# Expert output biases summed once per token, and gathers that pass over padding slots, in a mixture-of-experts kernel

## The chip, the cores and the metric

The kernel runs on one core of a Trainium2 chip. The metric is the device time of one execution in microseconds (us); the lower the better. Three executions of the kernel before gave a median of 3492.59 us.

## The reference, cut to what matters

A 512-token sequence of width 1024 passes through two layers of one network and then one layer of another. The last stage of the second is a mixture of 32 experts, of which each token uses four:

```python
def moe_ffn(h, router_w, router_b, w1, b1, w2, b2):
    ...
    top_val, top_idx = lax.top_k(logits, TOP_K)
    gates = jax.nn.softmax(top_val, axis=-1)
    ...
    def run_block(args):
        toks, e = args
        hb = x_pad[toks] @ w1[e] + b1[e]
        g_part = jnp.minimum(hb[..., ::2], SWIGLU_LIMIT)
        u_part = jnp.clip(hb[..., 1::2], -SWIGLU_LIMIT, SWIGLU_LIMIT)
        act = g_part * jax.nn.sigmoid(SWIGLU_ALPHA * g_part) * (u_part + 1)
        return act @ w2[e] + b2[e]

    y_slots = lax.map(run_block, (slot_tok.reshape(n_blocks, MOE_BLOCK), block_exp))
    y_slots = y_slots.reshape(n_slots, shp[-1]) * slot_gate[:, None].astype(xt.dtype)
    out = jnp.zeros((t + 1, shp[-1]), xt.dtype).at[slot_tok].add(y_slots)[:t]
```

A block is 128 slots of one expert. 512 tokens times 4 experts fill 2048 slots. A block that isn't full has padding slots, whose gate is 0. The sum over a token's four experts of gate times `b2[e]` is a product of the token's row of 32 gates with `b2`.

## The kernel before, in words

Everything up to the experts is one long static program: two layers of mixers and feed-forward (PE reads weight tiles that SP streams into a ring of 8 slots, `ring`), then the second network's mixer, its output projection (`out2`), the router and the tables of the experts. The experts are a loop with one turn for each block of 128 slots, and a last block written out without the work for a next one (`expert_block(i, more)` on PE, ACT and DVE, `route` on POOL, `loads` on SP). All engines run their own instruction streams in order and meet at semaphores.

One turn handles 24 weight tiles of 128x1024 (512 KB each): 0 to 7 and 8 to 15 are the two halves of `w1`, 16 to 23 are `w2`. Each tile passes through four hands:

- SP loads it into its ring slot (L427) as soon as DVE has finished with the tile that was there 8 tiles earlier (`s_lo`).
- ACT rounds it into a high part (`round_tile`, L1673), once the tile has landed and once PE has used the tile 6 earlier (`s_freed`; there are `SPLITS` = 6 pairs of parts).
- DVE subtracts to get the low part (`rest_of_tile`, L2514).
- PE multiplies: high by high, high by low, low by high, each in two halves of 512 columns, six matmuls a tile (`product`, L1150).

ACT and DVE run ahead of PE by up to six tiles. Between the tiles, in an order that is written out by hand in each engine's `expert_block`, lies the rest of a turn:

- PE adds a bias to each of its three products by a matmul of `sel` (the one-hot of the expert) with `biases` (`bias`, L1140): `b1` in two halves at L1164 and L1170, and `b2` at L1177.
- DVE makes the activation for each half (`swiglu`, L2542 to L2551), ACT its sigmoid (L1696), PE transposes it (`act_turned`, L1158), ACT rounds the transposed half (`act_hi`, L1702), and DVE subtracts (`act_lo`, L2557). PE waits for the first half of `act_lo` before tile 16 (L1178) and for the second before tile 20 (L1190).
- POOL works out which rows of `x_rows` the next block needs, gathers them with an indirect DMA (`gather`, L495), makes the one-hot matrices `pick` (L558) and `sel` (L561, after PE's `y_bias`), and adds the finished block to `y_rows` with an indirect DMA (L565).
- PE transposes the gathered rows (`x_turned`, L1101, first half after a wait for the gather at L1185), ACT and DVE round and subtract them (L1724, L2577).
- At the end of its turn ACT copies the block's output out of the banks, times the gates (`y_kept`, L1732), once PE has done the last tile (L1728). ACT's first tile of the next turn follows after that.

Padding slots: `row_next` gives them a row number of 512 or more. `x_rows` has 1024 rows, of which the upper 512 are zeros, written once by SP (L416, behind a wait for DVE at L414); the gather fetches them. The scatter adds the padding slots' zeros to the upper half of `y_rows`.

The prologue of the experts loads the biases into rows 0 to 63 of `biases` (POOL L479), clears, rounds and subtracts them (DVE L2388, ACT L1648, DVE L2394). The epilogue adds, for each of eight 128-wide slices of the output (`sums`, L1203 to L1214), the last block (`y_slot` times `last_rows`) and the four token blocks of `y_rows`, transposed.

## Time and profile before

| what | us |
|---|---|
| median of three runs | 3492.59 |
| the three runs | 3491.3 to 3494.47 |
| the profiled execution, its own time | 3500.01 |
| its span in the trace | 3498.2 |
| experts' loop, first block's first matmul to the last `y_kept` | 2257.3 to 3460.9 |

The page of the profile gives for the whole span:

```profile
DVE  4774655554854646555548970499999999999996
PEclk9989999999989999999999999899999999999999
DMA  5111344321101343321120013399999999999995
GB/s 201 49 31 34 102 136 137 116 90 60 42 25 55 119 133 122 115 91 54 49 74 17 25 52 111 125 355 357 356 374 362 354 365 368 357 367 367 357 366 203
```

A digit is the busy share of one fortieth of the span (87 us) in tenths. The last third is the loop of the experts. The profiled execution's own time is 1.8 us above its span, and 7.4 us above the median of the three runs.

### The profile page before, as it was taken

To read this page: it belongs to the slowest core of one execution; us is meant where nothing else is said; L and a number is where in the kernel's file an instruction comes from. 1 tells how busy PE (TensorE), PEld (TensorE's weight loads), DVE (VectorE), ACT (ScalarE), POOL (GpSimd) and SP (SyncE) were. 2 spreads that over 40 slices of the span, in tenths; PEclk is the share of its full clock that TensorE was granted. 3 is DMA by queue.
4 is the path that set the end of the run, shared out by engine and by line. 5 is a ranking of instruction groups with operands and counts; after the bars stand their busy time and mean duration, and the time that the engine had idled before them with its cause. 6 is when DMAs were issued, how large, how long until landed. Compare 5 with 4: busy or idle time off the path is not lost.

```text
span 3498.2 us, 42721 instructions
## 1 busy us (share of the span) xinstructions
PE 3311.9 (95%) x13182; PEld 2291.0 (65%) x13182; DVE 2430.2 (69%) x2947; ACT 1686.2 (48%) x2237; POOL 490.5 (14%) x625
## 2 busy tenths in 40 slices
PE   8979999999889999989999989799999999999997
PEld 3454587774353777755645654587888778878875
DVE  4774655554854646555548970499999999999996
ACT  3432433232441423232221140388888888888884
POOL 0000000000000000000000000143343443343341
PEclk9989999999989999999999999899999999999999
DMA  5111344321101343321120013399999999999995
GB/s 201 49 31 34 102 136 137 116 90 60 42 25 55 119 133 122 115 91 54 49 74 17 25 52 111 125 355 357 356 374 362 354 365 368 357 367 367 357 366 203
DMA packets 168012, 618.33 MB, mean 177 GB/s; under 512 B 18528, under 2 KB 18656, under 8 KB 167328
## 3 DMA queue, kind: packets, MB, share of 16 engines
q1 hardware_dynamic: 157232, 573.90, 45.5%
q0 software_dynamic: 10672, 43.00, 4.3%
q8 instruction: 66, 1.08, 0.1%
q14 instruction: 42, 0.34, 0.0%
HBM read 587.99 MB, written 28.84 MB: 176 GB/s over the span
## 4 chain that ended last, share of the span: by engine, by line
PE 72%; DVE 15%; issue 5%; ACT 3%; DMA 3%; DVEq 0%; POOL 0%; ACTq 0%; SPq 0%; POOLq 0%
PE bank L592 53%; PE bank L1150 16%; DVE w_part L2514 5%; DMA sb_ring<-in_w 3%; DVE sb_rstd L1770 1%; DVE sb_work L1808 1%; DVE sb_work L2547 1%; PE bank L1140 1%; DVE sb_work L2542 1%; ACT w_part L1673 1%; DVE sb_work L2544 1%; PE bank L1101 1%; PE bank L1158 1%; DVE sb_work L1956 0%; DVE sb_work L2270 0%
## 5 line engine op out<-in xcount | busy, mean ns | idle before, releaser
L2514 DVE TENSOR_TENSOR w_part<-sb_ring,w_part 128x1024 fp32r<-128x1024 f32 x762 | 890.4, 1225 | 66.1 <-ACT w_part L1673 65.4
L1673 ACT ACTIVATE w_part<-sb_ring 128x1024 fp32r<-128x1024 f32 x762 | 771.1, 1053 | 84.6 <-PE bank L1150 44.4
L1150 PE MATMUL bank<-w_part,xg_hi 128*128 128x512 f32 x2048 | 564.3, 397 | 0.0
L592 PE MATMUL bank<-h_hi,split_part 128*128 128x512 f32 x1408 | 445.0, 401 | 7.9 <-ACT h_hi L1431 7.9
L1150 PEld LDWEIGHTS bank<-w_part,xg_hi 128*128 128x128 f32 x2048 | 383.2, 188 | 88.8
L592 PE MATMUL bank<-sb_work,sb_ring 128*128 128x512 f32 (+2 forms) x840 | 315.4, 532 | 10.6 <-DVE sb_work L1786 10.6
L1150 PE MATMUL bank<-w_part,xg_lo 128*128 128x512 f32 x1024 | 321.3, 395 | 0.0
L592 PEld LDWEIGHTS bank<-h_hi,split_part 128*128 128x128 f32 x1408 | 266.4, 190 | 80.0 <-issue 15.6
L1150 PE MATMUL bank<-w_part,act_hi 128*128 128x512 f32 x1024 | 285.0, 400 | 1.7 <-DVE act_lo L2557 0.6
L592 PE MATMUL bank<-sb_hT,sb_ring 128*128 128x512 f32 x576 | 265.4, 619 | 11.7 <-ACT sb_hT L1251 11.7
L592 PE MATMUL bank<-h_lo,split_part 128*128 128x512 f32 x704 | 272.7, 394 | 0.0
L592 PEld LDWEIGHTS bank<-sb_work,sb_ring 128*128 128x128 f32 (+1 forms) x840 | 159.2, 192 | 156.7 <-issue 137.3
L592 PE MATMUL bank<-act_hi_ff,split_part 128*128 128x512 f32 x704 | 229.3, 407 | 5.7 <-DVE act_lo_ff L2129 5.7
L1424 ACT ACTIVATE split_part<-sb_ring 128x1024 fp32r<-128x1024 f32 x136 | 142.7, 1052 | 178.0 <-PE bank L592 178.0
L592 PE MATMUL bank<-sb_work 128*128 128x64 f32 (+7 forms) x1000 | 195.4, 400 | 31.2 <-DVE sb_work L2005 16.6
L1150 PEld LDWEIGHTS bank<-w_part,xg_lo 128*128 128x128 f32 x1024 | 192.8, 188 | 46.3
L592 PEld LDWEIGHTS bank<-sb_hT,sb_ring 128*128 128x128 f32 x576 | 114.4, 200 | 159.7 <-issue 157.6
L1150 PEld LDWEIGHTS bank<-w_part,act_hi 128*128 128x128 f32 x1024 | 187.6, 188 | 45.1 <-issue 4.1
L1481 ACT ACTIVATE sb_work<-bank 128x512 f32<-128x512 f32 x88 | 52.7, 599 | 310.5 <-PE bank L592 296.9
L592 PE MATMUL bank<-sb_xT,sb_ring 128*128 128x512 f32 (+2 forms) x416 | 181.5, 619 | 11.7 <-ACT sb_xT L1251 11.7
L592 PEld LDWEIGHTS bank<-sb_work 128*128 128x128 f32 (+3 forms) x1000 | 127.8, 207 | 82.6 <-issue 21.9
L2087 DVE TENSOR_TENSOR split_part<-sb_ring,split_part 128x1024 fp32r<-128x1024 f32 x136 | 165.9, 1221 | 19.5 <-ACT split_part L1424 19.1
(357 smaller groups left out, 4477.3 us busy)
## 6 DMA issues: line engine op xcount, KB each, us to landing
sb_ring<-in_w SPq DMA_DIRECT2D x768, 512.0 KB, 7.9
sb_ring<-in_wstream SPq DMA_DIRECT2D x304, 512.0 KB, 3.5
y_rows<-sb_padc POOLq DMA_DIRECT2D x1, 4096.0 KB, 17.5
sb_xT<-in_x SPq DMA_DIRECT2D x4, 512.0 KB, 6.8
x_rows<-sb_padc SPq DMA_DIRECT2D x1, 2048.0 KB, 10.2
residual<-sb_hT POOLq DMA_DIRECT2D x1, 2048.0 KB, 6.5
sb_hT<-residual POOLq DMA_DIRECT2D x1, 2048.0 KB, 8.1
x_rows<-sb_work SPq DMA_DIRECT2D x1, 2048.0 KB, 7.0
```

The costliest lines, as they stand in the source:

```text
L592: ins = nc.tensor.matmul(out, l, r, start=start, stop=stop)
L1101: ins = nc.tensor.transpose(out[:, k * P:(k + 1) * P], block_rows[:, (half * 4 + k) * P:(half * 4 + k + 1) * P], ident)
L1140: ins = nc.tensor.matmul(out[n][:], sel, biases[:, at + n * 512:at + (n + 1) * 512], start=True, stop=False)
L1150: ins = nc.tensor.matmul(out[n][:], l[:, k, :], r[:, n * 512:(n + 1) * 512], start=False, stop=(k, p) == (KD - 1, 2))
L1158: ins = nc.tensor.transpose(banks[6 + half][:, k * P:(k + 1) * P], u_part[:, half, k * P:(k + 1) * P], ident)
L1424: nc.scalar.activation(split_hi[t % NSPLIT], ring[:, n % RING, :], ACT.Copy).then_inc(act_done, did.up(("w_hi", l, t)))
L1481: nc.scalar.activation(ubuf[:, i % 4, 1:T + 1], bank_of("up", l, c, v)[:], ACT.Copy).then_inc(act_done, did.up(("free", "up", l, c, v), (" ...
L1673: nc.scalar.activation(w_hi[t % SPLITS], ring[:, t % RING, :], ACT.Copy).then_inc(s_hi, 1)
L1770: nc.vector.reciprocal(out, out).then_inc(dve_done, did.up())
L1808: nc.vector.scalar_tensor_tensor(out=dst[c], in0=a, scalar=b, in1=dst[c], op0=ALU.mult, op1=ALU.add).then_inc(dve_done, did.up())
L2087: nc.vector.tensor_tensor(split_lo[t % NSPLIT], ring[:, n % RING, :], split_hi[t % NSPLIT].bitcast(F32), ALU.subtract).then_inc(dve_done, ...
L2514: nc.vector.tensor_tensor(w_lo[t % SPLITS], ring[:, t % RING, :], w_hi[t % SPLITS].bitcast(F32), ALU.subtract).then_inc(s_lo, 1)
```

## The change

`b2` leaves the blocks. PE's bias matmuls of the third product go, and its first matmul starts the banks instead; POOL's `sel` waits for the second half of `b1` (`up_bias`) where it waited for `y_bias`. `b2` is loaded four times, into the four groups of 32 partitions of `b2_rows`. In the prologue PE transposes the gates (16 matmuls of 32 columns by 128, `gates_turned`), ACT copies them to `gate_t`. In the epilogue eight matmuls of 32 rows (`output_bias`) put gates times `b2` into the eight sums, six of them ahead of the wait for the last block, two at `m == 4`. Each uses one of the four groups of 32 rows.

The gather gets a bounds check at row 511, with rows beyond it left out and no error. So the zero rows of `x_rows`, their DMA, and the two waits for it go; POOL clears `block_rows` once before the loop. The last block, the scatter and `y_rows` stay as they are.

```diff
-ROWS_X = 2 * T
+ROWS_Y = 2 * T
...
-        biases = parts("biases", 1, 3 * D)[:, 0, :]
+        biases = parts("biases", 1, 2 * D)[:, 0, :]
+        b2_rows = region(D)
...
-        last_rows = turn_tables[:, 0, :]
+        last_rows, gate_t = turn_tables[:, 0, :], turn_tables[:, 1, :]
...
-                if n == RING + 1:
-                    sp.wait_ge(dve_done, when("zeros"))
-                    zeros = padc[:].rearrange("p a t -> p (a t)")[:, 0:D]
-                    sp.dma_start(x_rows[T:, :].rearrange("(g p) d -> p g d", p=P),
-                                 zeros.unsqueeze(1).to_broadcast([P, ROWS_X // P - TB, D])).then_inc(s_zero, 16)
...
             for half in range(2):
-                for at, name, n in ((0, "b1", 2 * D), (2 * D, "b2", D)):
-                    pool.dma_start(biases_raw[half * 32:half * 32 + 32, at:at + n], io[name]).then_inc(s_bias, 16)
+                pool.dma_start(biases_raw[half * 32:half * 32 + 32, :], io["b1"]).then_inc(s_bias, 16)
+            for i in range(P // EXPERTS):
+                pool.dma_start(b2_rows[i * EXPERTS:(i + 1) * EXPERTS, :], io["b2"]).then_inc(s_b2, 16)
...
                 nc.gpsimd.indirect_dma_start(out=block_rows, out_offset=None, in_=x_rows[:, :],
-                    in_offset=bass.IndirectOffsetOnAxis(ap=idx_next, axis=0)).then_inc(s_got, 16)
+                    in_offset=bass.IndirectOffsetOnAxis(ap=idx_next, axis=0), bounds_check=T - 1,
+                    oob_is_err=False).then_inc(s_got, 16)
...
-            pool.wait_ge(s_zero, 16)
             pool.wait_ge(s_rows, 16)
             pool.wait_ge(dve_done, when("biases"))
+            nc.gpsimd.memset(block_rows, 0.0).then_inc(pool_done, did.up(("block_rows_cleared",)))
+            pool.wait_ge(pool_done, did.n)
...
-                    pool.wait_ge(moe_pe_done, in_turn(i, "y_bias", more=more))
+                    pool.wait_ge(moe_pe_done, in_turn(i, "up_bias", more=more))
...
+            pe.wait_ge(dve_done, when("gates"))
+            for b in range(TB):
+                for i in range(P // EXPERTS):
+                    ins = nc.tensor.matmul(banks[3][i * EXPERTS:(i + 1) * EXPERTS, b * P:(b + 1) * P], gate[:, b, :],
+                                           ident, start=True, stop=True)
+            ins.then_inc(pe_done, did.up(("gates_turned",)))
...
+            pe.wait_ge(act_done, when("gates_kept"))
...
-                            ins = nc.tensor.matmul(out[n][:], l[:, k, :], r[:, n * 512:(n + 1) * 512], start=False,
-                                                   stop=(k, p) == (KD - 1, 2))
+                            ins = nc.tensor.matmul(out[n][:], l[:, k, :], r[:, n * 512:(n + 1) * 512],
+                                                   start=start and p == 0, stop=(k, p) == (KD - 1, 2))
...
-                bias(banks[2:4], D)
+                bias(banks[2:4], D).then_inc(moe_pe_done, turn_did.up(("up_bias",)))
...
                 pe.wait_ge(moe_act_done, in_turn(i, "y_kept", 1, back=1))
-                bias(banks[4:6], 2 * D).then_inc(moe_pe_done, turn_did.up(("y_bias",)))
                 pe.wait_ge(moe_dve_done, in_turn(i, "act_lo", 0, more=more))
                 for k in range(3):
-                    product(2 * KD + k, act_hi, act_lo, banks[4:6], k)
+                    product(2 * KD + k, act_hi, act_lo, banks[4:6], k, start=k == 0)
...
+            def output_bias(m):
+
+                r = slice(m % 4 * EXPERTS, (m % 4 + 1) * EXPERTS)
+                mm(outs[m][:], b2_rows[r, m * P:(m + 1) * P], gate_t[r, :], True, False)
+
+            pe.wait_ge(s_b2, 16 * (P // EXPERTS))
+            state["job"] = 0
+            outs = [bank("sums", m) for m in range(KD)]
+            for m in (0, 1, 2, 3, 6, 7):
+                output_bias(m)
             pe.wait_ge(dve_done, when("last_rows"))
-            state["job"] = 0
             for m in range(KD):
-                out = bank("sums", m)
+                out = outs[m]
                 if m % 4 == 0:
                     pe.wait_ge(moe_act_done, in_turn(last, "y_kept", m // 4, more=False))
-                mm(out[:], y_slot[:, m * P:(m + 1) * P], last_rows, True, False)
+                if m == 4:
+                    output_bias(4)
+                    output_bias(5)
+                mm(out[:], y_slot[:, m * P:(m + 1) * P], last_rows, False, False)
...
+            act.wait_ge(pe_done, when("gates_turned"))
+            nc.scalar.activation(gate_t, banks[3], ACT.Copy).then_inc(act_done, did.up(("gates_kept",)))
...
-                dve.wait_ge(s_zero, 16)
                 dve.wait_ge(s_put, 16)
```

The clearing, rounding and subtracting of `biases` (DVE L2388, ACT L1648, DVE L2394) shrink from 3072 to 2048 columns.

## Rows read from the trace of the kernel before

**Rows 1.** The page, part 1: busy time of each engine over the span.

```profile
PE 3311.9 (95%) x13182; PEld 2291.0 (65%) x13182; DVE 2430.2 (69%) x2947; ACT 1686.2 (48%) x2237; POOL 490.5 (14%) x625
```

**Rows 2.** Two turns as windows: length, busy PE, PEld, DVE, ACT, POOL, PEclk, DMA, GB/s.

```profile
2484.96:2523.42 38.46, 37.78 (x172) 30.14 (x171) 35.23 (x37) 30.76 (x37) 16.43 (x19) 1.00 0.97 353
2523.42:2560.49 37.07, 37.07 (x172) 30.25 (x171) 35.27 (x37) 30.92 (x37) 14.53 (x19) 1.00 1.00 372
```

**Rows 3.** Timeline of ACT (start, length, idle before), L1732, first and last of 32 pairs.

```profile
2297.03 1.25 ACT L1732 ACTIVATE sb_work<-bank,sb_work 128x512 f32<-128x512 f32 x2
...
3459.65 1.26 ACT L1732 ACTIVATE sb_work<-bank,sb_work 128x512 f32<-128x512 f32 x2 [7.18 <-PE bank L1150]
```

**Rows 4.** Timeline of PE in the shorter turn, around tile 20 and the turn's end.

```profile
2551.48 0.60 PE L1101 MATMUL bank<-sb_consts,sb_work 128*128 128x128 f32 x4
2551.84 1.18 PE L1150 MATMUL bank<-w_part,act_hi 128*128 128x512 f32 x4
...
2553.32 0.60 PE L1101 MATMUL bank<-sb_consts,sb_work 128*128 128x128 f32 x4
2553.67 1.19 PE L1150 MATMUL bank<-w_part,act_hi 128*128 128x512 f32 x4
...
2559.32 0.62 PE L1140 MATMUL bank<-biases,sel 128*128 128x512 f32 x2
2559.78 1.10 PE L1150 MATMUL bank<-w_part,xg_hi 128*128 128x512 f32 x4
```

**Rows 5.** Timeline of DVE in the shorter turn: first tile, second `act_lo`, last six tiles.

```profile
2527.07 8.04 DVE L2514 TENSOR_TENSOR w_part<-sb_ring,w_part 128x1024 fp32r<-128x1024 f32 x7 [1.47 <-ACT w_part L1673]
...
2552.86 0.68 DVE L2557 TENSOR_TENSOR act_lo<-bank,act_hi 128x512 fp32r<-128x512 f32 x1
...
2555.78 6.89 DVE L2514 TENSOR_TENSOR w_part<-sb_ring,w_part 128x1024 fp32r<-128x1024 f32 x6
```

**Rows 6.** Timeline of ACT in the shorter turn: `y_kept`, tile 12, the next `y_kept`.

```profile
2523.42 1.25 ACT L1732 ACTIVATE sb_work<-bank,sb_work 128x512 f32<-128x512 f32 x2
...
2532.67 1.06 ACT L1673 ACTIVATE w_part<-sb_ring 128x1024 fp32r<-128x1024 f32 x1 [0.33 <-PE bank L1150]
...
2560.49 1.25 ACT L1732 ACTIVATE sb_work<-bank,sb_work 128x512 f32<-128x512 f32 x2
```

**Rows 7.** Timeline of the longer turn: ACT's `y_kept`, tile 12, then DVE, PE at tile 20.

```profile
2484.96 1.25 ACT L1732 ACTIVATE sb_work<-bank,sb_work 128x512 f32<-128x512 f32 x2
...
2495.87 1.06 ACT L1673 ACTIVATE w_part<-sb_ring 128x1024 fp32r<-128x1024 f32 x1 [1.99 <-DMA sb_ring<-in_w]
...
2515.78 0.68 DVE L2557 TENSOR_TENSOR act_lo<-bank,act_hi 128x512 fp32r<-128x512 f32 x1
...
2516.59 1.19 PE L1150 MATMUL bank<-w_part,act_hi 128*128 128x512 f32 x4
```

**Rows 8.** POOL's gather in the shorter turn, and issue to landing of all 31.

```profile
2542.16 1.76 POOL L495 DMA_INDIRECT sb_work<-x_rows,sb_work  x1 [0.48 <-issue]
...
DMA to landing us min/median/max: 7.4/8.3/9.0
```

**Rows 9.** DMA: the gather's queue in 2504:2514, then all queues' slices in 2512:2522.

```profile
q0 software_dynamic: 144, 0.52, 13.1%
...
DMA  9999998989999998979999666698788446788998
```

**Rows 10.** PE's matmuls of 32 rows in 0:400, by shape: busy us, mean ns.

```profile
L592 PE MATMUL bank<-sb_work,sb_ring 32*128 32x512 f32 x4 | 2.0, 614 | 0.0
...
L592 PE MATMUL bank<-sb_work 32*128 32x384 f32 x16 | 1.9, 533 | 0.0
```

**Rows 11.** Timeline of PE at the end of the last block and the first sum.

```profile
3458.83 0.63 PE L1150 MATMUL bank<-w_part,act_lo 128*128 128x512 f32 x2
3460.39 1.13 PE L592 MATMUL bank<-sb_turn_tables,sb_work 128*128 128x512 f32 x2 [0.94 <-ACT sb_work L1732]
```

**Rows 12.** Timeline of PE: its first matmul of the experts' loop.

```profile
2257.34 1.22 PE L1140 MATMUL bank<-biases,sel 128*128 128x512 f32 x2 [7.39 <-POOL sb_work L530]
```

More of the change, by code:

```diff
@@ L149, in build @@
         s_bias = sem("expert_biases_loaded")
-        s_zero = sem("token_rows_cleared")
+        s_b2 = sem("output_biases_loaded")
         s_rows = sem("token_rows_stored")
@@ L169, in build @@
         banks = [bank_pairs[i // 2][:, i % 2 * 512:(i % 2 + 1) * 512] for i in range(8)]
-        x_rows = nc.dram_tensor("x_rows", (ROWS_X, D), F32, kind="Internal").ap()
-        y_rows = nc.dram_tensor("y_rows", (ROWS_X, D), F32, kind="Internal").ap()
+        x_rows = nc.dram_tensor("x_rows", (T, D), F32, kind="Internal").ap()
+        y_rows = nc.dram_tensor("y_rows", (ROWS_Y, D), F32, kind="Internal").ap()
         residual = nc.dram_tensor("residual", (P, KD * T), F32, kind="Internal").ap()
@@ L338, in build @@
         u_part = rows(2, D // 2)
-        biases_raw = work[:, raw_at:raw_at + 3 * D]
+        biases_raw = work[:, raw_at:raw_at + 2 * D]
         idents = region(EXPERTS)
@@ L432, in _ @@
                 sp.wait_ge(act_done, when("h2_row", b, 1))
-            sp.dma_start(x_rows[0:T, :].rearrange("(b p) d -> p b d", p=P), h2[:]).then_inc(s_rows, 16)
+            sp.dma_start(x_rows.rearrange("(b p) d -> p b d", p=P), h2[:]).then_inc(s_rows, 16)
             sp.wait_ge(dve_done, when("table"))
@@ L461, in _ @@
                            padc[:].rearrange("p a t -> p (a t)")[:, 0:D].unsqueeze(1).to_broadcast(
-                               [P, ROWS_X // P, D])).then_inc(s_put, 16)
+                               [P, ROWS_Y // P, D])).then_inc(s_put, 16)
             did = Count("pool", found)
@@ L1142, in bias, with product @@
                     return ins
-                def product(t, left_hi, left_lo, out, k):
+                def product(t, left_hi, left_lo, out, k, start=False):
                     pe.wait_ge(s_lo, i * MOE_TILES + (t + 1))
@@ L1643, in _ @@
                     c)).then_inc(act_done, did.up(("free", "yt", c), ("mixed", c)))
-            act.wait_ge(s_bias, 64)
+            act.wait_ge(s_bias, 32)
             act.wait_ge(dve_done, when("biases_cleared"))
-            nc.scalar.activation(biases[0:64, :], biases_raw[0:64, :], ACT.Copy).then_inc(act_done, did.up(("biases_hi",)))
+            nc.scalar.activation(biases[0:64, 0:2 * D], biases_raw[0:64, :], ACT.Copy).then_inc(act_done, did.up(("biases_hi",)))
             for k in range(KD):
@@ L2387, in _ @@
             dve.wait_ge(pe_done, when("full", "yt", XC - 1))
-            nc.vector.memset(biases.bitcast(F32), 0.0).then_inc(dve_done, did.up(("biases_cleared",)))
+            nc.vector.memset(biases[:, 0:2 * D].bitcast(F32), 0.0).then_inc(dve_done, did.up(("biases_cleared",)))
             for m in range(KD):
@@ L2393, in _ @@
                     dve.wait_ge(act_done, when("biases_hi"))
-                    nc.vector.tensor_tensor(biases[32:64, :], biases_raw[32:64, :], biases[32:64, :].bitcast(F32),
+                    nc.vector.tensor_tensor(biases[32:64, 0:2 * D], biases_raw[32:64, :], biases[32:64, 0:2 * D].bitcast(F32),
                         ALU.subtract).then_inc(dve_done, did.up(("biases",)))
@@ L2440, in _ @@
             nc.vector.tensor_tensor(gate, gate, gate_sum.unsqueeze(2).to_broadcast([P, TB, EXPERTS]),
-                ALU.mult).then_inc(dve_done, did.up())
+                ALU.mult).then_inc(dve_done, did.up(("gates",)))
             dve.wait_ge(pe_done, when("full", "rank"))
```

## The prediction, made before the changed kernel was run

> **What bounds the kernel now.** The page's busy times come first. PE looks like the bound, 95% of the span, with DVE far behind [rows 1]. That is a mean over stages with other limits, so the next view is windows of exactly one turn of the experts' loop, from one `y_kept` to the next [rows 2]. The reader is to see that turns come in two kinds, 37.07 and 38.46 us long, with the same work in them. The loop's mean lies between: from the first pair of `y_kept` to the last are 31 turns in 3459.65 - 2297.03 = 1162.62 us, 37.50 each [rows 3]. In the shorter turn PE is busy for all of the 37.07 us, but DVE for 35.27, and DMA's share is 1.00: three resources are near their end at once, and busy shares can't tell which one sets the turn. The timelines can.
>
> PE, shorter turn [rows 4]: before tile 20 PE transposes the second half of the gathered rows at 2553.32 and starts tile 20 at 2553.67, 0.35 later. The transposes of the first half, which have no wait behind them, take 2551.84 - 2551.48 = 0.36. So PE reached tile 20 without waiting.
>
> DVE, shorter turn [rows 5]: it idles once, 1.47 us, before the turn's first tile at 2527.07 (3.65 after `y_kept`, since ACT has the copy and a tile to do first). From there to the end of the last group at 2562.67 the timeline shows no idle time. In this unbroken chain the second `act_lo`, for which tile 20 waits, ends at 2552.86 + 0.68 = 2553.54. PE's tile 20 starts 0.13 behind it.
>
> The same pair in the longer turn [rows 7]: `act_lo` ends at 2515.78 + 0.68 = 2516.46, tile 20 starts at 2516.59, again 0.13 behind. And from the end of `act_lo` to the next `y_kept` it is 2560.49 - 2553.54 = 6.95 us in the shorter turn [rows 5, 6] and 2523.42 - 2516.46 = 6.96 in the longer [rows 6, 7]. **So both turns are timed by DVE's chain**: `y_kept`, ACT's first tile, DVE's unbroken work up to the second `act_lo` (30.12 us), then 6.95 us of four tiles on PE, ACT's last tile and `y_kept`. In the shorter turn PE arrives at the same moment by its own road.
>
> What makes a turn longer: ACT's tile 12 starts 10.91 us after `y_kept`, behind a wait of 1.99 for DMA, where it stands at 9.25 in the shorter turn [rows 6, 7]. 1.66 late, less a little slack, comes out as 1.39 in the turn. Over the loop such lateness is 37.50 - 37.07 = 0.43 a turn, 13.3 us in 31 turns.
>
> **The change, part by part.**
>
> *The two bias matmuls of the third product.* A pair takes 2559.78 - 2559.32 = 0.46 us of PE [rows 4], 14.3 us over 31 turns, more than the whole of the 0.2% (7 us) that a measurement of this kernel can tell from no change. But they stand before tile 16, and PE's time before tile 20 is what the DVE chain covers. Without them PE arrives at tile 20 at 2553.21 instead of 2553.67 and waits for an `act_lo` that is ready at 2553.54 and lets it start at 2553.67 as before. For the gain to get through, DVE's chain would have to start or run earlier. Its start is anchored to `y_kept`, its tiles up to 21 need only parts that PE frees before the place of the removed pair, and it has no idle time to give back. I take 0.01 a turn, -0.3 us; the bounds are 0 and -14.3. The last block has a wait of its own at tile 20 and gives nothing.
>
> Matmul busy time, read alone, names PE as the bound [rows 2]. The Trainium skill (Perfetto Trace Analysis, Identifying the Most-Contended Engine) calls that a bad measure, since matmuls are pipelined, and goes by weight loads for PE and by occupancy for the others, of which the highest is to be worked on first. By the first reading the sum here would be -14; by the rule DVE, at 35.27 of 37.07 against 30.25 for weight loads [rows 2], is the engine to relieve, and the removal on PE gives 0.
>
> *The gather.* `sel` waits for `up_bias` instead of `y_bias`, eight tiles earlier on PE; POOL makes it behind the four `pick`s, so an earlier signal frees nothing: 0, and a `sel` made sooner would be used no sooner. The gather was issued at 2542.16 and used at 2551.48 [rows 4, 8], 9.32 later; it lands 8.3 after issue, 9.0 at most [rows 8]. PE now comes for it 0.46 sooner, but may be held until the old moment without cost, since it only waits at tile 20 anyway. 2048 of 4096 slots are filled, so half of the rows go. The queue's 0.52 MB took 13.1% of 16 engines for 10 us, 1.31 us [rows 9]; half is 0.65 us of DMA a turn. What could that buy? Only the 13.3 us of late tiles. The lateness sits at tile 12, 8 to 11 us into a turn, beside the scatter. The gather is issued 2542.16 - 2523.42 = 18.7 us into the turn and lands at 27, when little is left before the second `act_lo` at 30. Between that place and the next tile 12 the DMA engines have slack: from about 2517.5 on, 6 us before the `y_kept` at 2523.42, quarters of a microsecond fall to 4 to 7 tenths [rows 9]. Backlog is worked off there, and 0.65 us less of it mostly widens a gap. I take -1 us; bounds 0 and -13.3.
>
> *Prologue.* PE waits 7.39 us before the loop's first matmul [rows 12]. In it fit 16 short transposes; from the pace of 0.09 us of the 128-column transposes (0.36 for four, [rows 4]) that is 1.5 us, and ACT's copy of 512 columns under 0.7 us (a `y_kept` pair is 1.25, [rows 6]). Both end before POOL's one-hots. POOL's clear of `block_rows` stands after the work that PE waits for, and 15 us before its next wait on ACT ends. The two more loads, the smaller `biases` and the missing 2 MB of zeros lie beside PE work that runs on: 0, bounds -1 and +1.
>
> *Epilogue.* PE idles 0.94 us before the first sum [rows 11], and from there to the end PE's work is the path. The six `output_bias` ahead of it: where matmuls of 32 rows use one group of rows, four of 512 columns take 2.0 us, 0.5 each; where four groups follow each other, sixteen of 384 columns take 1.9, 0.12 each [rows 10]. The new ones cycle through the groups. Side by side: four of 512 columns in 4 x 0.12 x 512/384 = 0.64, two more in 0.5: 1.14, less 0.94: +0.2. Two at `m == 4`: +0.5. Sum **+0.7**. One after another: 6 x 0.5 - 0.94 + 2 x 0.5 = +3.1, the upper bound; the lower is +0.3, with the six hidden and the last two side by side. I take +0.7, since the rows with different groups are the same pattern.
>
> **Sum**: -0.3 - 1 + 0 + 0.7 = -0.6 us on the profiled execution's 3500.01, so 3499.4. That execution lies 7.4 above the median of the runs, 3492.59; on the median it is **3492.0 us**.
>
> **The rivals.**
>
> *A, PE bounds the turn.* For it: PE 37.07 busy of 37.07, and no wait at tile 20 in the short turns. Against it: the constant 6.95 behind `act_lo` in turns of both kinds. It would give 3492.6 - 14.3 + 0.7 = 3479.0.
>
> *B, the lighter gather takes away the late tiles.* For it: DMA's share is 1.00 in the short turn, and lateness is all that makes turns longer. Against it: the slack between gather and tile 12. If two thirds of the 13.3 go: 3492.6 - 9 + 0.7 = 3484.
>
> *C, slower: the checked gather lands too late.* POOL computes the addresses in software, and the check may lengthen that. The margin is 9.32 - 8.3 = 1.0 us from issue to use [rows 4, 8]; past it every microsecond delays tile 19, tile 20 and the turn, and 31 turns make 31 us. If it lands 2 us later than now less the 0.65 saved, the turn loses 0.35: 3492.6 + 11 + 0.7 = 3504. From 1.65 us of added address work on it decides. Against it: half of the rows are gone, and the whole gather instruction is only 1.76 us on POOL.
>
> *D, the change doesn't do what it says*: rows out of bounds still cost a packet each. Then the gather's part is 0 instead of -1, and the time is 3493.0, inside the forecast.
>
> **How the numbers follow.** Forecast with D: 0.63 for within 0.2% (3485.6 to 3499.6). A 0.08 and B 0.16, both on the faster side, of B some that falls short of 7 us but about as much luck from late tiles falling elsewhere: faster 0.24. C 0.08, and 0.05 for more late tiles, since tile 12 is decided by tenths of a microsecond: slower 0.13. The range reaches down to most of B and leaves out A, 3481; and up to the serial epilogue with a few more late turns, 3499. The forecast's own range is 3489 to 3496.
>
> **What would show it.** Short turns still 37.05 to 37.07 long; in them PE now waits some 0.4 us at tile 20 for DVE's `act_lo`, a wait that the page before doesn't show there; 6.95 us from `act_lo` to `y_kept`; no L1140 of the third product; half of the gather's packets; the same number of turns with tile 12 late; first sum 0.2 later. Wrong if short turns fall to 36.6 (A), if long turns vanish (B), or if PE waits at the gathered rows (C).

## The result, and the profile after

The changed kernel takes 3500.52 us (median of 8 runs, 3496.07 to 3510.85), the kernel before on the same chip 3492.86 (8 runs): ratio 1.0026, interval 1.0014 to 1.0038, 7.7 us slower. The prediction was 3492.0, in a range from 3481 to 3499: the kernel is slower than that, by 8.5 us against the forecast and 1.5 against the end of the range. The same kernel as a new program gave 1.0022 (1.0013 to 1.0031).

The changed kernel's page, engines' busy times (as [rows 1]), the software queue, the third product's group:

```profile
PE 3306.4 (95%) x13166; PEld 2275.4 (65%) x13166; DVE 2426.6 (69%) x2947; ACT 1685.9 (48%) x2238; POOL 502.0 (14%) x628
...
q0 software_dynamic: 10768, 35.04, 3.8%
...
L1156 PE MATMUL bank<-w_part,act_hi 128*128 128x512 f32 x1024 | 285.1, 400 | 3.7 <-DVE act_lo L2575 0.9
```

The reader is to see that the group of the expert products (L1156) now has a wait for DVE's `act_lo`, which is that of tile 20. For queue 0 the DMA view of the whole execution is of use, the kernel before first:

```profile
DMA packets 168012, 618.33 MB, mean 177 GB/s; under 512 B 18528, under 2 KB 18656, under 8 KB 167328
q0 software_dynamic: 10672, 43.00, 4.3%
```

```profile
DMA packets 167580, 608.27 MB, mean 174 GB/s; under 512 B 20552, under 2 KB 20680, under 8 KB 166896
```

Queue 0 moved 35.04 MB where it had moved 43.00, so the bytes of the padding rows are gone. Its packets are not: 10672 before, 10768 now, and 2024 more of all packets are under 512 bytes, about the 1984 rows that 31 gathers skip at 64 each. A skipped row is still a packet, of 4 bytes in the trace and 9 ns where a row of 4 KB takes 164. A gather takes 0.69 us of the 16 engines instead of 1.32.

Three turns of the changed kernel as windows, columns as [rows 2]:

```profile
2447.33:2485.65 38.32, 37.31 (x170) 29.74 (x169) 35.23 (x37) 30.87 (x37) 15.78 (x19) 1.00 0.98 354
2485.65:2522.73 37.08, 36.98 (x170) 29.79 (x169) 35.22 (x37) 31.15 (x37) 16.23 (x19) 1.00 1.00 356
2522.73:2559.81 37.08, 36.98 (x170) 29.80 (x169) 35.23 (x37) 31.12 (x37) 16.54 (x19) 1.00 1.01 366
```

The short turn is 37.08 as before, with two matmuls fewer. Its PE timeline, answering [rows 4], and behind it DVE's line for the second `act_lo` [rows 5]:

```profile
2550.44 0.60 PE L1100 MATMUL bank<-sb_consts,sb_work 128*128 128x128 f32 x4
2550.80 1.19 PE L1156 MATMUL bank<-w_part,act_hi 128*128 128x512 f32 x4
...
2552.29 0.60 PE L1100 MATMUL bank<-sb_consts,sb_work 128*128 128x128 f32 x4
2552.99 1.19 PE L1156 MATMUL bank<-w_part,act_hi 128*128 128x512 f32 x4
```

```profile
2552.18 0.68 DVE L2575 TENSOR_TENSOR act_lo<-bank,act_hi 128x512 fp32r<-128x512 f32 x1
```

From the second transposes to tile 20 it is 0.70 us now, 0.35 before, and 0.36 behind the first transposes: PE arrives earlier and waits 0.34, until 0.13 behind the end of `act_lo`, as predicted.

A longer turn is as before too: tile 12 waits for its DMA and starts 10.77 behind `y_kept`, as in [rows 7]. Timeline of ACT:

```profile
2447.33 1.25 ACT L1751 ACTIVATE sb_work<-bank,sb_work 128x512 f32<-128x512 f32 x2
...
2458.10 1.06 ACT L1690 ACTIVATE w_part<-sb_ring 128x1024 fp32r<-128x1024 f32 x1 [1.49 <-DMA sb_ring<-in_w]
```

First and last `y_kept`, as [rows 3]:

```profile
2295.88 1.25 ACT L1751 ACTIVATE sb_work<-bank,sb_work 128x512 f32<-128x512 f32 x2
...
3457.46 1.26 ACT L1751 ACTIVATE sb_work<-bank,sb_work 128x512 f32<-128x512 f32 x2 [7.17 <-PE bank L1156]
```

The loop is 1161.58 us here, 1162.62 in the profiled execution before. This says little: the number of long turns differs from execution to execution (below), and both spans happen to be 3498.2. The prologue ends 1.15 us sooner here and 0.92 later in the repetition (first `y_kept` at 2297.95); over all runs below that moment moves between 2295.1 and 2299.0, so no cost shows. The final sums tell more. PE's timeline there, against [rows 11]:

```profile
3457.19 3.05 PE L591 MATMUL bank<-sb_turn_tables,sb_work 32*128 32x512 f32 x14
3460.09 1.05 PE L591 MATMUL bank<-sb_consts,sb_work 128*128 128x128 f32 x8
...
3465.34 1.02 PE L591 MATMUL bank<-sb_turn_tables,sb_work 128*128 128x512 f32 x2
3466.20 1.05 PE L591 MATMUL bank<-sb_consts,sb_work 128*128 128x128 f32 x8
...
3468.04 2.18 PE L591 MATMUL bank<-sb_turn_tables,sb_work 32*128 32x512 f32 x6
3470.06 1.05 PE L591 MATMUL bank<-sb_consts,sb_work 128*128 128x128 f32 x8
```

A token-row matmul (two records) takes 3466.20 - 3465.34 = 0.86 to its follower. With six `output_bias` ahead of it the same step takes 2.90: 2.04 for six, 0.34 each. With two it takes 2.02: 1.16 for two, 0.58 each. The output's DMA, by SP's timeline, the kernel before first:

```profile
3491.55 0.34 SPq L453 DMA_DIRECT2D out_h<-sb_xT  x1
```

```profile
3491.53 0.34 SPq L449 DMA_DIRECT2D out_h<-sb_xT  x1
```

From the last `y_kept` to it: 3491.55 - 3459.65 = 31.90 before, 3491.53 - 3457.46 = 34.07 after. This stretch is called the tail below. **The final sums cost 2.17 us**, in every profiled execution alike (34.07 or 34.08 with all eight output biases there, 31.89 or 31.90 without). That leaves 5.5 of the 7.7 us.

### The profile page after: what moved, and what is told of

Its sections match the earlier page's. It is cut to its first block, busy times and chain, and to the rows that moved or that the text cites. A ratio compares the mean times of both kernels' runs of the same rounds, so it can differ in the third digit from the quotient of the medians.

```text
span 3498.2 us, 42721 instructions
## 1 busy us (share of the span) xinstructions
PE 3306.4 (95%) x13166; PEld 2275.4 (65%) x13166; DVE 2426.6 (69%) x2947; ACT 1685.9 (48%) x2238; POOL 502.0 (14%) x628
## 3 DMA queue, kind: packets, MB, share of 16 engines
q0 software_dynamic: 10768, 35.04, 3.8%
## 4 chain that ended last, share of the span: by engine, by line
PE 64%; DVE 19%; issue 8%; DMA 4%; ACT 4%; DVEq 0%; POOL 0%; ACTq 0%; SPq 0%; POOLq 0%
PE bank L591 52%; PE bank L1156 9%; DVE w_part L2532 7%; DMA sb_ring<-in_w 4%; DVE sb_rstd L1789 1%; DVE sb_work L1827 1%; DVE sb_work L2565 1%; ACT w_part L1690 1%; DVE sb_work L2560 1%; DVE sb_work L2562 1%; DVE act_lo L2575 0%; DVE sb_work L2288 0%; DVE sb_work L1974 0%; DVE sb_work L2332 0%; PE bank L1100 0%
## 5 line engine op out<-in xcount | busy, mean ns | idle before, releaser
L1156 PE MATMUL bank<-w_part,xg_hi 128*128 128x512 f32 x2048 | 564.1, 397 | 0.0
L1156 PEld LDWEIGHTS bank<-w_part,xg_hi 128*128 128x128 f32 x2048 | 383.2, 188 | 89.2
L591 PE MATMUL bank<-sb_work,sb_ring 128*128 128x512 f32 (+2 forms) x840 | 315.4, 531 | 10.6 <-DVE sb_work L1805 10.6
L1156 PE MATMUL bank<-w_part,xg_lo 128*128 128x512 f32 x1024 | 321.2, 395 | 0.0
L1156 PE MATMUL bank<-w_part,act_hi 128*128 128x512 f32 x1024 | 285.1, 400 | 3.7 <-DVE act_lo L2575 0.9
L1156 PEld LDWEIGHTS bank<-w_part,xg_lo 128*128 128x128 f32 x1024 | 192.6, 188 | 46.5
L1156 PEld LDWEIGHTS bank<-w_part,act_hi 128*128 128x128 f32 x1024 | 187.4, 188 | 50.8 <-issue 9.8
```

Of the source, the lines that this page charges most:

```text
L591: ins = nc.tensor.matmul(out, l, r, start=start, stop=stop)
L1156: ins = nc.tensor.matmul(out[n][:], l[:, k, :], r[:, n * 512:(n + 1) * 512], start=start and p == 0, stop=(k, p) == (KD - 1, 2))
```

## The experiments

Each ratio is against the kernel before on the same chip, beside the runs compared. "Loop" is first to last `y_kept` of the profiled execution, "long" its turns over 37.9 us of 31, "DMA" what ACT idled for a tile's DMA in the loop (in the line that rounds tiles).

| kernel | median us | ratio, interval | loop | long | DMA us |
|---|---|---|---|---|---|
| before (first profile) | 3492.86 | | 1162.6 | 9 | 36.4 |
| after (first profile) | 3500.52 | 1.0026 (1.0014-1.0038) | 1161.6 | 8 | 30.7 |
| again_before | 3496.34 | 0.9999 (0.9990-1.0008) | 1157.4 | 4 | 28.4 |
| again_after | 3502.41 | 1.0022 (1.0013-1.0031) | 1157.1 | 5 | 25.3 |
| check_only | 3496.98 | 1.0002 (0.9993-1.0011) | 1163.6 | 9 | 36.2 |
| check_only_again | 3500.50 | 1.0019 (1.0010-1.0028) | 1166.5 | 11 | 38.4 |
| bias_only | 3497.49 | 1.0009 (0.9998-1.0021) | 1164.2 | 11 | 32.2 |
| bias_only_again | 3497.49 | 1.0009 (1.0000-1.0019) | 1155.4 | 3 | 25.1 |
| after_pe_filled | 3502.43 | 1.0027 (1.0016-1.0038) | 1156.5 | 4 | 23.7 |
| after_no_sums_bias | 3499.58 | 1.0018 (1.0007-1.0028) | 1165.6 | 11 | 34.5 |
| before_no_scatter | 3485.22 | 0.9978 (0.9969-0.9987) | 1147.8 | 0 | none |
| after_no_scatter | 3482.45 | 0.9968 (0.9959-0.9978) | 1142.7 | 0 | none |
| before_scatter_checked | 3495.60 | 1.0005 (0.9996-1.0014) | 1159.1 | 7 | 17.0 |
| after_scatter_checked | 3496.44 | 1.0008 (0.9999-1.0018) | 1159.6 | 7 | 21.1 |
| before_scatter_late | 3488.33 | 0.9982 (0.9973-0.9991) | 1149.7 | 0 | 10.6 |
| after_scatter_late | 3490.79 | 0.9978 (0.9968-0.9988) | 1150.6 | 0 | 14.4 |
| before_lo_early | 3504.60 | 1.0027 (1.0015-1.0039) | 1161.7 | 4 | 55.9 |
| after_lo_early | 3508.70 | 1.0034 (1.0022-1.0047) | 1170.7 | 13 | 71.6 |
| after_lo_early_bias_moved | 3502.02 | 1.0026 (1.0015-1.0038) | 1166.9 | 8 | 70.2 |
| after_lo_early_scatter_late | 3542.96 | 1.0115 (1.0094-1.0136) | 1222.2 | 15 | 14.9 |

**Chance first.** again_before and again_after are the two kernels unchanged.

> The kernel before, once more, for a second profile of it. Its first profile was of an execution of 3500.0 us, above all eight timed ones (3486.7 to 3494.5). If that was chance, this profile shows a loop some 5 to 7 us shorter than 1162.6, with fewer turns over 37.9 us than the 9 of 31. If profiling itself costs the time, it shows about 3500 again. Ratio 1.000.

> The changed kernel, once more, for a second profile. Ratio to the kernel before 1.002 to 1.003 as measured (7 to 9 us). If the added time is the epilogue and more late turns: y_kept of the last block to the output's DMA 34.1 us again (31.9 before), and 8 or more turns over 37.9 us, shortest turns 36.9 to 37.1.

The first came as expected. Of the second the ratio and the tail did (34.08), but 5 turns are long where 8 or more were expected. Two executions of one and the same kernel have loops 3 to 9 us apart in the table. So one profiled execution can't show 5 us; medians of some ten runs can, and so can kernels without long turns.

**The two halves.** check_only is the kernel before with the bound on the gather:

```diff
-                    in_offset=bass.IndirectOffsetOnAxis(ap=idx_next, axis=0)).then_inc(s_got, 16)
+                    in_offset=bass.IndirectOffsetOnAxis(ap=idx_next, axis=0), bounds_check=T - 1,
+                    oob_is_err=False).then_inc(s_got, 16)
...
+            nc.gpsimd.memset(block_rows, 0.0).then_inc(pool_done, did.up(("block_rows_cleared",)))
```

> The kernel before with the bounds check of the gather and the clearing of block_rows alone; biases stay in the blocks. If the partial gather is what costs (its rows sit on fewer DMA engines, so that tiles finish less evenly): slower by 4 to 6 us, with more late turns. If the gather is harmless as I predicted: within 2 us of before, rather faster by 1.

> The kernel before with the bound on the gather alone, once more, because its first 12 runs (1.0002, 0.9993 to 1.0011) can't tell 1 us from 4. If the lighter gather carries the rest of the loss, 1.001 or more; if it costs nothing, 0.999 to 1.0005.

bias_only is the kernel after with the old gather:

```diff
-                    in_offset=bass.IndirectOffsetOnAxis(ap=idx_next, axis=0), bounds_check=T - 1,
-                    oob_is_err=False).then_inc(s_got, 16)
+                    in_offset=bass.IndirectOffsetOnAxis(ap=idx_next, axis=0)).then_inc(s_got, 16)
...
-            nc.gpsimd.memset(block_rows, 0.0).then_inc(pool_done, did.up(("block_rows_cleared",)))
```

> The changed kernel with the gather as it was (all rows, zero rows in x_rows). If the bias part is what costs: all of the 7 to 8 us, of which 2.2 is the epilogue and -1 the prologue, the rest in the loop, though its shortest turns are no longer than before. If it is the gather: +1 to +2 us, the epilogue alone.

> The kernel after with the gather unchecked over 1024 rows as before, once more (first 1.0009, 0.9998 to 1.0021). If the bias part carries the whole loss, 1.002 or more; if it is the final sums alone, 1.0006.

The bias half costs 0.0009 twice, 3.1 us, of which the final sums are 2.2. The gather half gave 0.0002 and 0.0019, on different chips: 0.7 and 6.6 us, and the two intervals barely meet, at 0.0010. With their mean, about 4, the halves add up to 7, what the change costs. But on the chip where both halves and the whole were run side by side they add up to 0.0011 against 0.0022 for the whole. How the loss divides between the halves isn't settled.

**Is it PE's earlier arrival?** after_pe_filled puts two matmuls of the removed form back (`sel` waits for `y_bias` again):

```diff
                 pe.wait_ge(moe_act_done, in_turn(i, "y_kept", 1, back=1))
+                for n in range(2):
+                    ins = nc.tensor.matmul(banks[4 + n][:], sel, biases[:, n * 512:(n + 1) * 512], start=True, stop=True)
+                ins.then_inc(moe_pe_done, turn_did.up(("y_bias",)))
```

> The kernel after with two matmuls of the removed form (sel against 512 columns of biases) put back at the old place of the third product; their result is thrown away by the start of tile 16, so that only their 0.46 us on PE and the old signal for sel are restored. Theory 1 (PE's earlier arrival changes the order of work around it and with that the number of turns with a late tile 12): the 4 to 5 us that the final sums don't explain go, ratio 1.0006 to 1.0012. Theory 2 (they come from the lighter gather or the prologue, or were chance): ratio stays at 1.0018 to 1.0026.

1.0027, where theory 1 had 1.0006 to 1.0012: it falls. With PE's time and the old signal restored the loss is still there, so PE's earlier arrival isn't what costs. after_no_sums_bias leaves the eight `output_bias` out:

```diff
-            for m in (0, 1, 2, 3, 6, 7):
-                output_bias(m)
...
-                if m == 4:
-                    output_bias(4)
-                    output_bias(5)
-                mm(out[:], y_slot[:, m * P:(m + 1) * P], last_rows, False, False)
+                mm(out[:], y_slot[:, m * P:(m + 1) * P], last_rows, True, False)
```

> This kernel leaves out the eight output_bias matmuls of the final sums, so the output biases are in no output; all else is the kernel after. Theory (the final sums carry a third of the loss): from the last y_kept to the output's DMA issue 31.9 us as before instead of 34.1, and the ratio 1.0022 falls by 2.2 / 3493 = 0.0006 to about 1.0016. Rival (the final sums carry it all, since each ran alone in the earlier runs by chance): the ratio falls to 1.000. If it stays at 1.0022 or more, the tail is not what a slower run shows.

The tail is 31.90 again. The ratio, 1.0018 (1.0007 to 1.0028), is clear of the rival's 1.000; 0.0006 less than before is inside its interval and can't be told from no gain.

**Taking the scatter away.** Both kernels, the scatter-add replaced by a DMA of 64 bytes:

```diff
-                    nc.gpsimd.indirect_dma_start(out=y_rows[:, :], out_offset=bass.IndirectOffsetOnAxis(ap=idx_cur,
-                        axis=0), in_=y_slot, in_offset=None, compute_op=ALU.add).then_inc(s_put, 16)
+                    pool.dma_start(y_rows[0:1, 0:16], y_slot[0:1, 0:16]).then_inc(s_put, 16)
```

> This kernel leaves out the scatter-add of each block's output to the token rows (a DMA of 64 bytes takes its place, so that the waits stay), so only the last block's outputs reach the sums; all else is the kernel before. Theory (turns are longer than 37.07 us only where the scatter gets ahead of tile 12): every turn 37.07 to 37.1, the loop 31 x 37.08 = 1149.5 us against 1157 to 1164, the time 8 to 13 us less, ratio 0.9965 to 0.998, and the spread between executions shrinks to a few us. Rival (late tiles come from DMA's load as such): long turns stay.

> The same leaving out of the scatter-add on the kernel after. Theory 1 (of the 7 us that the change costs, 2.2 are the final sums and the rest are more or longer late turns): 2.2 us over before_no_scatter, and no more. Theory 2 (something in the prologue or the short turns that the profiles don't show costs the rest): 7 us over before_no_scatter, as with the scatter.

The first expectation held. Of the second neither theory did: both have the changed kernel slower. Of all runs these tell the most. No turn is long, and the spread is 3 us instead of 12 to 15. Without the scatter the changed kernel is the **faster** one, by 3485.22 - 3482.45 = 2.8 us. The loops differ by 1147.8 - 1142.7 = 5.1 in its favour, the final sums by 2.2 against it. Timelines show why, first before_no_scatter: DVE's second `act_lo`, PE's second transposes, tile 20.

```profile
2512.36 0.68 DVE L2556 TENSOR_TENSOR act_lo<-bank,act_hi 128x512 fp32r<-128x512 f32 x1
...
2512.99 0.60 PE L1100 MATMUL bank<-sb_consts,sb_work 128*128 128x128 f32 x4
...
2513.35 1.18 PE L1149 MATMUL bank<-w_part,act_hi 128*128 128x512 f32 x4
```

`act_lo` has ended at 2513.04; tile 20 starts 0.31 later, 0.36 behind the transposes: PE doesn't wait, it sets this turn of 37.07. The same in after_no_scatter:

```profile
2511.56 0.68 DVE L2574 TENSOR_TENSOR act_lo<-bank,act_hi 128x512 fp32r<-128x512 f32 x1
2511.73 0.60 PE L1099 MATMUL bank<-sb_consts,sb_work 128*128 128x128 f32 x4
...
2512.37 1.19 PE L1155 MATMUL bank<-w_part,act_hi 128*128 128x512 f32 x4
```

Tile 20 stands 0.13 behind `act_lo`, so DVE sets a turn of 36.90. Its `act_lo` ends 2512.24 - 2482.29 = 29.95 behind `y_kept`; with the scatter it is 2552.86 - 2522.73 = 30.13. So with the scatter DVE's chain is 0.18 longer (in before_no_scatter it is 2513.04 - 2483.09 = 29.95 too), and that is just what hid PE's gain: the kernel before sat on a tie of two engines at 37.07.

The scatter therefore costs the kernel before about 8 us (3493.21 - 3485.22), all of it in turns over 37.07. For the kernel after the runs with it were on other chips, so the ratios are used: 1.0026 or 1.0022 less 0.9968, 19 to 20 us, of which 31 x 0.18 = 5.6 are in the short turns and 13 to 15 in longer ones. **By this account the change pays 5 to 7 us more in turns that are longer than the short ones.** It is an account by elimination, from medians: the single profiled executions don't show it, with 8 and 5 long turns in the kernel after and 9 and 4 in the kernel before.

**A lighter scatter.** Both kernels with `bounds_check=T - 1, oob_is_err=False` on the scatter-add too.

> The kernel after with the bound T - 1 on the scatter-add too, so that padding slots are passed over in both. Theory (scatter beside tile 12): the scatter's 2.64 us of 16 DMA engines fall to 1.3, fewer turns are late, the time falls by 3 to 10 us against the kernel after: ratio 0.9995 to 1.0015 against before. Rival (the address work on POOL or the number of rows doesn't matter): 1.0024 as the kernel after.

> The kernel before with the bound T - 1 on the scatter-add alone (the gather stays whole). Theory: 3 to 10 us less than the kernel before, ratio 0.997 to 0.999, faster than both kernels, since it has the lighter scatter and not the 2.2 us in the final sums. Rival: no difference.

Half of the scatter's rows gone: the kernel after gains 5 to 6 us by the ratios, as expected, the kernel before nothing, where 3 to 10 us were expected. 7 turns of 31 are still long in both, inside the 4 to 9 of the kernels with the whole scatter. ACT's waits for DMA do fall, from 28.4 and 36.4 us to 17.0 in the kernel before. So half the bytes take away waits, but not the long turns.

**A later scatter.** Three one-column additions on POOL ahead of it, in either kernel:

```diff
+                    for _ in range(3):
+                        after(turn_did, 3, (moe_pool_done, own_turn(i, turn_did)))
                     nc.gpsimd.indirect_dma_start(out=y_rows[:, :], out_offset=bass.IndirectOffsetOnAxis(ap=idx_cur,
```

> The kernel before with three more one-column additions on POOL ahead of the scatter-add, which is then issued 1 us later (3.4 us into the turn instead of 2.4), DVE and PE unchanged. Theory (the slower lo_early kernels are slower because their scatter is issued at 3.0 to 3.5 and meets tile 12 more often): ratio 1.001 to 1.003, more turns over 37.5. Rival (the moment of issue doesn't matter): 1.000.

> The kernel after with the same three additions on POOL ahead of the scatter-add. Theory (what the change costs beyond the final sums comes only through turns whose tile 12 falls behind the scatter): issued 0.9 us later, the scatter lets tile 12 pass in nearly every turn, and what remains between this kernel and before_scatter_late is the final sums: 3488.3 + 2.2 = 3490.5, ratio 0.9988 to 0.999, spread of a few us. Rival (the lighter gather costs 4 us by another way): 3494 or more, ratio 1.000.

The first expectation has the wrong sign: issued later, the scatter does *less* harm. POOL's timeline in the kernel before, `y_kept` at 2523.42:

```profile
2524.75 0.90 POOL L504 TENSOR_TENSOR sb_work<-sb_work 128x1 f32<-128x1 f32 x1 [11.11 <-ACT sb_work L1732]
2525.81 1.65 POOL L565 DMA_INDIRECT y_rows<-sb_work  x1 [0.16 <-POOL sb_work L504]
```

And in before_scatter_late, `y_kept` at 2518.69:

```profile
2520.02 1.71 POOL L504 TENSOR_TENSOR sb_work<-sb_work 128x1 f32<-128x1 f32 x4 [11.12 <-ACT sb_work L1734]
2522.02 1.65 POOL L567 DMA_INDIRECT y_rows<-sb_work  x1 [0.29 <-issue]
```

Issue moves from 2.39 to 3.33 behind `y_kept`. The load that tile 12 waits for is issued by SP at the same place in both, 1.22 behind `y_kept`; before, then before_scatter_late:

```profile
2524.64 0.33 SPq L427 DMA_DIRECT2D sb_ring<-in_w  x1
```

```profile
2519.91 0.33 SPq L427 DMA_DIRECT2D sb_ring<-in_w  x1
```

So its head start on the scatter is 1.17 us before and 2.11 here. ACT's group for the tiles in 2300:3435 (busy, mean, idle before and its releasers), of before, before_no_scatter, before_scatter_late:

```profile
L1673 ACT ACTIVATE w_part<-sb_ring 128x1024 fp32r<-128x1024 f32 x727 | 735.4, 1053 | 78.5 <-PE bank L1150 39.4 <-DMA sb_ring<-in_w 36.4
```

```profile
L1672 ACT ACTIVATE w_part<-sb_ring 128x1024 fp32r<-128x1024 f32 x736 | 738.8, 1052 | 59.1 <-PE bank L1149 58.0
```

```profile
L1675 ACT ACTIVATE w_part<-sb_ring 128x1024 fp32r<-128x1024 f32 x734 | 741.8, 1053 | 64.1 <-PE bank L1152 51.4 <-DMA sb_ring<-in_w 10.6
```

The DMA entry is the lateness: 36.4 with the scatter at 2.4, none without it, 10.6 with it at 3.3, and no long turn is left. So it is a race of the scatter with tile 12: from issue to landing the load of tile 12 takes 6.5 to 9.8 us in the kernel before, over 8 in 11 turns of 31; 6.5 to 7.7 without the scatter; 6.0 to 7.8 with the later one. ACT can take the tile 9.26 behind `y_kept`, 8.03 behind the load's issue. In that setting the changed kernel takes 3490.79 (3490.5 was expected) and the unchanged one 3488.33. Their difference, 2.5, fits the final sums, but they ran on different chips; by the ratios the changed kernel is 1.4 us the faster, give or take some 5. What the pair shows is that the loss beyond the sums is gone or small. Both are faster than the kernel before, by 0.9978 (0.9968 to 0.9988) and 0.9982 (0.9973 to 0.9991), and compute all of it.

**An earlier `act_lo`.** DVE makes the second `act_lo` one tile sooner:

```diff
-                for t in range(2 * KD + SPLITS - 1, 2 * KD + SPLITS + 1):
-                    rest_of_tile(i, t)
-                rest_of_act(1)
-                rest_of_tile(i, 2 * KD + SPLITS + 1)
+                rest_of_tile(i, 2 * KD + SPLITS - 1)
+                rest_of_act(1)
+                for t in range(2 * KD + SPLITS, 2 * KD + SPLITS + 2):
+                    rest_of_tile(i, t)
```

> Theory (DVE's chain to the second act_lo times the short turns, and the removal of the third product's bias on PE is real but covered by it): with the second act_lo one tile earlier on DVE it no longer waits behind 1.2 us of tile 21 and 22, only for ACT's act_hi, some 0.6 us earlier. PE's wait of 0.4 at tile 20 goes, short turns fall from 37.06 to 36.6 to 36.7, and 31 turns give 10 to 14 us: ratio 0.997 to 0.999 against the kernel before, where the kernel after has 1.0022. Rival (DMA times the turn): short turns stay at 37.0, ratio 1.002.

> The same reordering on the kernel before. Theory: there PE arrives at tile 20 as late as DVE, with 37.06 us of work of its own in the turn, so act_lo earlier gives at most 0.1 a turn: short turns 36.9 to 37.06, ratio 0.999 to 1.000. Rival (DVE alone sets it, PE has slack): as much as in the kernel after, ratio 0.996.

after_lo_early_bias_moved also has, in the last block:

```diff
                 product(2 * KD + 3, act_hi, act_lo, banks[4:6], 3)
+                if not more:
+                    for m in range(4):
+                        output_bias(m)
```

> after_lo_early with the output biases of the first four row groups issued in the last block, ahead of PE's wait at tile 20. Theory: at 0.41 us each they cost PE 1.6 us there less what is left of that wait (0.3 to 0.9), and the first sum starts behind two of them instead of six, inside its wait for y_kept: 1 us or less under after_lo_early, tail from y_kept 32.9 instead of 34.1. Rival: they shift the last block by as much as they save, no difference.

Windows of a longer and a short turn of after_lo_early:

```profile
2485.15:2523.48 38.33, 37.03 (x170) 29.70 (x169) 35.32 (x37) 30.98 (x37) 15.30 (x19) 1.00 0.96 340
2523.48:2560.21 36.73, 36.73 (x170) 29.77 (x168) 35.56 (x37) 30.87 (x36) 15.03 (x19) 1.00 1.01 376
```

The shortest turns are near what the theory said: 36.73 with the change, 37.06 without it. This settles the tie. Removing PE's pair alone leaves the short turns at 37.08, an earlier `act_lo` alone at 37.07, and both together give 36.73. The times are not what it said, for ACT's waits for a tile's DMA double (71.6 and 55.9 us). DVE ends its turn later and frees the slot for tile 12 later; POOL's small addition is held as well, 1.83 us where it had taken 0.90. After_lo_early, `y_kept` at 2485.15, first SP's load of tile 12, then POOL:

```profile
2487.30 0.33 SPq L423 DMA_DIRECT2D sb_ring<-in_w  x1
```

```profile
2486.48 1.83 POOL L502 TENSOR_TENSOR sb_work<-sb_work 128x1 f32<-128x1 f32 x1 [10.73 <-ACT sb_work L1751]
2488.47 1.64 POOL L564 DMA_INDIRECT y_rows<-sb_work  x1 [0.16 <-POOL sb_work L502]
```

The scatter goes out at 3.32, as late as in before_scatter_late, but the load goes out at 2.15, and its head start is 1.17 again. With it the load takes 6.1 to 9.8 us, over 8 in 11 turns, as in the kernel before (before_lo_early: up to 10.3, over 8 in 4 turns). So, as far as these profiles show, what the load suffers goes by the distance of the two issues, and not by the scatter's own moment. And since ACT still wants the tile at 9.26, a load that leaves 0.92 later is late more often: in 25 turns of 31, against 11.

Moving four biases saved 0.9 us of the tail (33.2; 32.9 was expected). The medians fell by 6.7 us and the ratio by 0.0008, 2.8 us, which is within its interval: the tail alone shows what the move gives.

after_lo_early_scatter_late adds the three additions to that.

> after_lo_early_bias_moved with the three additions ahead of the scatter-add. Theory (there the short turns are 36.75 to 36.85, and only the late tiles hid that; with the scatter out of tile 12's way they show): loop 31 x 36.9 = 1144 us, tail 33, time 3482 to 3486, ratio 0.997, faster than every other version that computes all. Rival (with turns of 36.8 the scatter, now issued 4.3 us in, meets the next tiles or the DMA engines are full): ratio 1.000 or more.

1.0115, the worst of all. POOL's timeline in a turn whose `y_kept` is at 2533.40, then PE's:

```profile
2534.74 3.60 POOL L502 TENSOR_TENSOR sb_work<-sb_work 128x1 f32<-128x1 f32 x4 [10.72 <-ACT sb_work L1757]
2538.49 2.45 POOL L566 DMA_INDIRECT y_rows<-sb_work  x1 [0.16 <-POOL sb_work L502]
...
2556.59 1.91 POOL L492 DMA_INDIRECT sb_work<-x_rows,sb_work  x1
```

```profile
2564.92 0.93 PE L1102 MATMUL bank<-sb_consts,sb_work 128*128 128x128 f32 x4 [3.77 <-DMA sb_work<-x_rows,sb_work]
```

Four additions take 3.60 us instead of 1.71: DVE idles only 0.54 there, and 1.48 in before_scatter_late. The scatter leaves at 5.09, the next gather at 23.2 instead of 18.9, and PE waits 3.77 for its rows: a turn of 42.15. This is rival C's mechanism, a gather that lands too late. In the loop PE waits 51.2 us in all for gathered rows here, and 0.3 or less in every other run.

## Why the prediction was wrong, point by point

- *The third product's bias, 0 to -0.3 us in the loop*: right for this kernel, short turns 37.08 and a wait of 0.34 at tile 20. "Both turns are timed by DVE's chain" was true by hundredths only, so the right number owes something to luck. Without the scatter the old turn is PE's, 37.07, and the removal gives 0.17 a turn. Rival A was half there. The Trainium skill's advice to work on the engine with the highest occupancy (Perfetto Trace Analysis, Identifying the Most-Contended Engine) picks DVE, and the removal on PE gave nothing, as it has it; but relieving DVE alone gave nothing either (before_lo_early), and in before_no_scatter, where DVE is still the busier by that measure, the engine to relieve is PE.
- *What starts DVE's chain*: "3.65 after `y_kept`, since ACT has the copy and a tile to do first" leaves out a term. Between the two stands a load of ACT's function tables, in the shorter turn of the kernel before:

```profile
2524.68 1.28 ACT L1673 ACT_TABLE_LOAD   x1
```

  It doesn't change the forecast, since it is there in both kernels, but these 1.28 us are part of DVE's chain in 30 of 31 turns. No run takes them away.
- *The lighter gather, -1 us, bounds 0 and -13.3*: **this step failed.** It is the only term that priced the late tiles, and its bounds allowed no loss. Measured, the change loses some 5.5 us beyond the final sums. With the scatter gone it gains 5.1 in the loop instead, and with a later scatter the loss is gone or small. The gather alone gave +0.7 and +6.6. The reasoning "0.65 us less of it mostly widens a gap" concerned the mean load, but lateness is the outcome of a race decided by tenths of a microsecond, and a change of DMA timing can move such a race either way. A bound on the slow side was due.
- *The final sums, +0.7*: **mis-sized**, +2.17 measured, in the bounds of 0.3 and 3.1. The steps were 2.04 for six and 1.16 for two, where 1.14 and 0.5 had been taken, so the first sum starts 1.03 later behind `y_kept` and not 0.2. "The same pattern" as the sixteen of 384 columns was not the same price; why is not shown.
- *Prologue 0*: right within what the runs can tell.
- *Rival C*: the gather's instruction takes 1.75 us on POOL in the median, 1.63 in the first profile before and 1.75 in the second, and lands 8.1 after issue (8.3 before). It is not why the change is slower.
- *Rival D and the sign "half of the gather's packets"*: a row out of bounds does still cost a packet, but one of 4 bytes. The DMA time fell as forecast, by 0.63 us a gather, and the count of packets did not.
- *Slower 0.13*: the chance for more late turns, 0.05, was too small for a term whose swing between two executions of one kernel is 3 to 9 us.

With the measured terms: 2.2 for the sums, some 4 for the gather's part (the mean of two that disagree), 1 or less for the rest: 7 on 3493, or 3500.

**What stays open.** That the loss beyond the sums needs the scatter where it is, is shown: it is gone without the scatter, and gone or small with the later one. That it lies in longer turns follows by elimination, since tail, prologue and short turns are equal or accounted for; no profile shows more of them. That the checked gather is what makes them is only likely: its two measurements disagree. How it would do so is not shown; its transfers sit far from tile 12, and short turns with and without it are equal.

## What to carry to other kernels

Where turns of a loop come in two lengths, find what race separates them before pricing a change: a cut that leaves the mean load lower may still lose more races. Measure the distance between the issues of the two transfers: with 1.17 us of head start the load of tile 12 took over 8 us in 3 to 14 turns of 31, and up to 10.5; with 2.11 in none of 31 in one kernel, and in 4 of 31 and up to 8.9 in the other. Moving the rival transfer (here the scatter-add, by one microsecond, with three tiny additions) was worth more than either half of the change. And work that is removed from inside a covered stretch, but added to a tail that nothing covers, must be priced at the tail's own rates.

## What the runs showed of the hardware

- Six fp32 matmuls of 32 rows by 512 columns, each on another group of rows than its neighbour, took 0.34 us each, two took 0.58 each. Four on the four groups in turn, in the last block of after_lo_early_bias_moved, took 3458.05 - 3456.98 = 1.07, 0.27 each. Sixteen of 384 columns had taken 0.12 each [rows 10].

```profile
3456.98 1.14 PE L591 MATMUL bank<-sb_turn_tables,sb_work 32*128 32x512 f32 x8
3458.05 1.20 PE L1165 MATMUL bank<-w_part,act_hi 128*128 128x512 f32 x4
```

- A row that the gather's bound passes over stayed a packet, of 4 bytes and 9 ns instead of 4 KB and 164 ns.
- Halving the rows of the scatter-add left 7 turns of 31 long, while ACT's waits for DMA fell to 17.0 us.
- A one-column addition on POOL takes 0.19 us by itself and mostly 0.9 to 1.3 beside DVE's subtractions of tiles, of 1.22 each. Ahead of the scatter it took 1.83 in after_lo_early, beside two subtractions without a gap, and once 6.36; four in a row took 1.71 where DVE idled for 1.48 beside them, 3.60 where it idled for 0.54. The Trainium skill (SBUF — State Buffer, Terms) has DVE and GpSimd arbitrate for one exclusive pair of ports, the loser blocked for the whole instruction; the timelines agree, and here the wait can last for more than one of DVE's instructions.
